# One block for the projection stage and the page steps, an earlier stick-breaking chain, and router weights turned by TensorE

## What is computed

```python
def stick_breaking(q, k, v, q_pos, k_pos):
    z = einsum('bqhd,bkhd->bhqk', q, k) * SCALE
    causal = k_pos[None, :] < q_pos[:, None]
    log_stay = where(causal, log_sigmoid(-z), 0.0)
    later = cumsum(log_stay, axis=3, reverse=True) - log_stay
    a = where(causal, exp(log_sigmoid(z) + later), 0.0)
    return einsum('bhqk,bkhd->bqhd', a, v)

def forgetting(q, k, v, cq, ck, q_pos, k_pos):
    z = einsum('bqhd,bkhd->bhqk', q, k) * SCALE + cq[..., :, None] - ck[..., None, :]
    p = softmax(where(causal, z, -inf), axis=-1)
    return einsum('bhqk,bkhd->bqhd', p, v)

def hier_moe(u, w_rg, b_rg, w_re, b_re, w_gate, w_up, w_down):
    lg = u @ w_rg + b_rg                      # 4 groups
    le = einsum('td,gde->tge', u, w_re) + b_re  # 4 x 8 experts
    ...
```

## Time and profile before

| | us |
|---|---|
| median of 3 runs | 1610.4 (1608.38 to 1613.99) |
| the profiled execution | 1617.14 |
| its span in the profile | 1615.2 |
| PE busy | 1275.5 (79%) |
| DVE busy | 668.7 (41%) |
| ACT busy | 230.6 (14%) |
| moved by DMA | 576.64 MB, 357 GB/s over the span |
| mean granted TensorE clock | 0.882 |

### The profile page before, as it was taken

How to read it: one execution, slowest core, us unless ns; L and a number is a source line. 1 busy time by engine, 2 the same in 40 slices (tenths; PEclk the granted TensorE clock), 3 DMA queues, 4 the chain that set the end, 5 groups by cost and what they waited for, 6 DMA issues and landing times. The chain is left out here.

```text
span 1615.2 us, 24640 instructions
## 1 busy us (share of the span) xinstructions
PE 1275.5 (79%) x7826; PEld 811.5 (50%) x7827; DVE 668.7 (41%) x4780; ACT 230.6 (14%) x454; POOL 62.4 (4%) x107
## 2 busy tenths in 40 slices
PE   5996679887969889847999776789867787767782
PEld 3775356655646656514777432355434444334451
DVE  3544655666557657659734654020100000000004
ACT  2100101212202213211010021010110001100011
POOL 1000000000000000001000000000010000000000
PEclk8998789899979989967999885799998889988997
DMA  9868599999989999999989899999999999999974
GB/s 329 235 221 325 176 397 394 397 396 394 357 334 379 395 366 395 389 388 371 360 335 361 316 364 353 411 377 411 422 399 381 381 388 388 372 375 382 369 332 167
DMA packets 188252, 576.64 MB, mean 357 GB/s; under 512 B 28697, under 2 KB 88906, under 8 KB 170218
## 3 DMA queue, kind: packets, MB, share of 16 engines
q1 hardware_dynamic: 116432, 507.82, 81.2%
q10 hardware_dynamic: 67282, 58.55, 11.0%
q0 software_dynamic: 4432, 9.05, 1.7%
HBM read 568.74 MB, written 17.77 MB: 363 GB/s over the span
## 5 line engine op out<-in xcount | busy, mean ns | idle before, releaser
L129 DVE CUSTOM_DVE_ANT_0 ws<-ws,xgT 128x128 f32<-128x128 f32 x1792 | 386.5, 281 | 90.2 <-issue 36.5
L1877 PE MATMUL bank<-ws,xgT 128*64 128x256 f32 x1024 | 260.4, 419 | 108.2 <-DMA ws<-in_w_expert_up 104.6
L932 PE MATMUL bank<-xn,ws 128*128 128x264 f32 x1152 | 297.0, 414 | 58.3 <-DMA ws<-in_w_in 58.3
L932 PEld LDWEIGHTS bank<-xn,ws 128*128 128x128 f32 x1152 | 228.0, 203 | 156.5 <-DMA ws<-in_w_in 66.9
L1879 PE MATMUL bank<-ws,xgT 128*64 128x256 f32 x1024 | 260.6, 419 | 0.0
L1877 PEld LDWEIGHTS bank<-ws,xgT 128*64 128x64 f32 x1024 | 152.9, 152 | 205.8 <-issue 120.5
L2076 DVE COPY gu<-bank 128x256 f32<-128x256 f32 x32 | 13.6, 424 | 391.0 <-PE bank L1879 391.0
L917 PE MATMUL bank<-ws,PR 128*32 128x512 f32 x1024 | 150.7, 668 | 21.2 <-DMA ws<-in_cache_fox_v 17.5
L1879 PEld LDWEIGHTS bank<-ws,xgT 128*64 128x64 f32 x1024 | 152.7, 152 | 0.0
L129 DVE DVE_READ_ACCUMULATOR2_ANT Z<- 128x1 f32 x1792 | 137.0, 76 | 0.0
L1898 PE MATMUL bank<-ws,hT 128*32 128x512 f32 x1024 | 115.7, 604 | 12.7 <-ACT xgT L1975 12.5
(11 more groups left out here) (409 smaller groups left out, 968.9 us busy)
## 6 DMA issues: line engine op xcount, KB each, us to landing
ws<-in_cache_sb_k SPq DMA_DIRECT2D x128, 512.0 KB, 8.1
ws<-in_cache_fox_k SPq DMA_DIRECT2D x128, 512.0 KB, 10.1
ws<-in_cache_sb_v SPq DMA_DIRECT2D x128, 512.0 KB, 7.6
ws<-in_cache_fox_v SPq DMA_DIRECT2D x128, 512.0 KB, 9.9
ws<-in_w_expert_gate SPq DMA_DIRECT2D x32, 2048.0 KB, 17.8
ws<-in_w_expert_up SPq DMA_DIRECT2D x32, 2048.0 KB, 24.9
ws<-in_w_expert_down SPq DMA_DIRECT2D x32, 2048.0 KB, 25.8
ws<-in_w_in ACTq DMA_DIRECT2D x16, 2048.0 KB, 30.2
```

Of the source, the lines that this page charges most:

```text
L129: ins = dve.tensor_tensor_reduce(k, k, qb[:, (g * H + h) * HD:(g * H + h + 1) * HD], 1.0, 0.0, ALU.mult, ALU.add, Z[:, n % 2, g, h, t:t + 1])
L932: mm = pe.matmul(out[:, 0:T], w[:, c, m * P:(m + 1) * P], xn[:, c, :], start=(c == 0), stop=(c == KC - 1))
L1877: pe.matmul(bank[2 * k][0:SLOTS, 0:256], lhs, ws[:, wg, c * 256:(c + 1) * 256], start=(c == 0), stop=(c == KC - 1))
```

## The change

1. The first block's streams become functions (`class start`) that each engine runs at the beginning of the second block. The meeting of the engines, the clearing of the first set of semaphores and the wait for the `lf` stores between the two go. The first set is cleared at the end of the merged block, so three sets are cleared there instead of two. The stores of `lf` move forward, behind query chunk 6, and are waited for in step 8.
2. The stick-breaking chain of sample 0 moves to the time when the fox half of its pages is being scored: the softplus on ACT stands behind `head(4)`, the sum and scan on DVE ahead of the fox half, the two sum matmuls on PE behind `head(6)`, `ts` behind the first fox half page, and its exponential on ACT behind the fox queries. The softmax part stays at the start of the steps. There PE first turns the maximum, then broadcasts sample 1's queries. POOL's clearing of `PR` runs once the gate logits are made.
3. The router weights are loaded by SP as rows (16 partitions with 4 KB each) ahead of the query chunks, and PE turns them with 36 small transposes; DVE copies them to `wr`. The gains also move to SP, ahead of the chunks; `wf`, `bf` and `br` are issued by ACT later.
4. Buffers of the first stage now lie inside those of the second (`blk`, `PR`, `osum`, `zs`, `zr`, `ts`, `zx`), and several semaphores are shared.

The diff, cut to the core:

```diff
@@ SP
                 for t in (2, 0, 1):
                     ...
                     sp.dma_start(xrow[0:n, t, :], src).then_inc(A[f"x{t}"], 16)
+                for i, (name, r0, r1) in enumerate((("norm_attn_g", 0, 16), ...)):
+                    sp.dma_start(grow[r0:r1, :], a[name][0].rearrange("(c p) -> c p", p=P)).then_inc(A["g_in"], 16)
+                for g in range(NG):
+                    sp.dma_start(wrow[g], a["w_router_expert"][0, g].rearrange("(c p) e -> c (p e)", p=P)).then_inc(A["wr_in"], 16)
+                sp.dma_start(wrow[4], a["w_router_group"][0].rearrange("(c p) g -> c (p g)", p=P)).then_inc(A["wr_in"], 16)
                 for n in range(4):
                     q_chunk(n)
...
                 q_chunk(6)
+                sp.wait_ge(A["fgc"], FG["lf"])
+                sp.dma_start(logf_p[0, 0]..., lf[:, 0:2, :]).then_inc(A["lst"], 16)
+                sp.dma_start(logf_s[0]..., lf[0:NB, 2, :]).then_inc(A["lst"], 16)
...
-                sp.wait_ge(A["lf"], 1)
-                sp.dma_start(logf_p[0, 0]..., lf[:, 0:2, :]).then_inc(A["lst"], 16)
-                sp.dma_start(logf_s[0]..., lf[0:NB, 2, :]).then_inc(A["lst"], 16)
-                sp.wait_ge(A["lst"], 32)
@@ ACT
                 head(4)
+                act.wait_ge(A["hused"], PAGES)
+                own.step(nc.scalar.activation(zs[:, :], Z[:, 0, 0, :, :]..., ACT.Abs, scale=SCALE))
+                own.step(nc.scalar.activation(zs[:, :], zs[:, :], ACT.Exp, scale=-1.0))
+                nc.scalar.activation(zs[:, :], zs[:, :], ACT.Ln, bias=1.0).then_inc(S["ssl"], 1)
                 head(5)
                 head(6)
                 partial(3)
                 act.wait_ge(S["bcast"], 1)
                 for i in range(2, 4):
                     nc.scalar.activation(qb[:, i * 512:(i + 1) * 512], bank[i][:, :], ACT.Copy).then_inc(S["qb"], 1)
+                act.wait_ge(S["pad"], 1)
+                act.wait_ge(S["ts"], 1)
+                nc.scalar.activation(PR[:, 0, :, 0:H]..., ts[:, :]..., ACT.Exp).then_inc(S["w"], 1)
@@ PE
+                pe.wait_ge(A["wr_in"], 16 * (NG + 1))
+                for e in range(NE):
+                    g, i = divmod(e, EPG)
+                    pe.transpose(bank[3][:, e * KC:(e + 1) * KC], wrow[g]...[:, i, :], ident[0:KC, 0:KC])
+                for g in range(NG):
+                    mm = pe.transpose(bank[2][:, g * KC:(g + 1) * KC], wrow[4]...[:, g, :], ident[0:KC, 0:KC])
                 pe.wait_ge(A["rc"], 1)
...
                 head(6)
+                pe.wait_ge(A["fgc"], FG["ctc"])
+                pe.wait_ge(S["ssp"], 1)
+                pe.matmul(bank[1][:, P:2 * P], tri_ge[:, :], sp_h[:, :, 1:PAGES + 1], start=True, stop=False)
+                pe.matmul(bank[1][:, P:2 * P], ones[:, :], run[:, :, 0:PAGES], start=False, stop=True).then_inc(A["fg"], 1)
                 partial(7)
...
-            pe.wait_ge(S["pad"], 1)
+            start.tensor(pe)
+            sample_max(0)
+            pe.wait_ge(A["q_evac"], 12)
             broadcast_queries(pe, S, bank[4:8], lastq, qpart, 1)
-            sample_max(0)
-            sample_sums(0)
+            pe.wait_ge(S["diag"], 1)
+            pe.matmul(bank[CH][:, 256:256 + H], ones[0:H, :], diag[:, :], start=True, stop=True).then_inc(S["C2"], 1)
@@ ACT, ahead of the steps
+            start.scalar(act)
+            act.wait_ge(S["zx"], 1)
+            nc.scalar.activation(PR[:, 1, :, 0:H]..., zx[:, :]..., ACT.Exp).then_inc(S["w"], 1)
             copy_queries(nc, act, S, bank[4:8], qb, 1)
-            sample_softplus(0)
-            act.wait_ge(S["pad"], 1)
-            sample_weights(0)
@@ DVE
+                own.step(dve.tensor_scalar(zr[:, :], z_sb, SCALE, 0.0, ALU.mult, ALU.max))
+                dve.wait_ge(S["ssl"], 1)
+                own.step(dve.tensor_tensor(sp_h[:, :, 1:PAGES + 1], zr..., zs..., ALU.add))
+                dve.tensor_tensor_scan(run..., seg..., sp_h..., 0.0, ALU.mult, ALU.add).then_inc(S["ssp"], 1)
                 for i in range(PAGES, 2 * PAGES):
                     score_half(i)
+                    if i == PAGES:
+                        dve.wait_ge(A["fg"], FG["c2s"])
+                        dve.scalar_tensor_tensor(out=ts[:, :], in0=z_sb, scalar=SCALE, in1=bank[1][:, P:2 * P], ...).then_inc(S["ts"], 1)
-        done_with(nc, A)
...
         attention_and_route(...)
+        done_with(nc, A)
         done_with(nc, S)
         done_with(nc, C)
@@ DVE, ahead of the steps
+            start.vector(dve)
+            dve.wait_ge(S["kused"], PAGES)
+            own.step(dve.scalar_tensor_tensor(out=zx[:, :], in0=flat(Z[:, 0, 1, :, :]), scalar=SCALE, in1=FB[:, 0, :], ...))
+            dve.tensor_reduce(mxp[:, :], by_head(zx[:, :]), AX, ALU.max).then_inc(S["mx"], 1)
+            dve.wait_ge(S["mxT"], 1)
+            own.step(dve.tensor_reduce(m8[:, :], bank[CH][0:H, 0:P], AX, ALU.max))
+            dve.tensor_scalar(diag[:, :], ident[0:H, 0:H], m8[:, 0:1], None, ALU.mult).then_inc(S["diag"], 1)
+            dve.wait_ge(S["C2"], 1)
+            own.step(dve.tensor_copy(MX[:, 0, :], bank[CH][:, 256:256 + H]))
+            dve.tensor_tensor(by_head(zx[:, :]), by_head(zx[:, :]), over(MX[:, 0, :], PAGES), ALU.subtract).then_inc(S["zx"], 1)
+            for p in range(PAGES, LEAD):
+                score_page(dve, S, kring, qb, Z, p)
```

More of the change, by code:

```diff
@@ new lines, in hybrid_step @@
+        sp_h = sb("sp_h", [P, H, PAGES + 1], where=bctx)
+        run = sb("run", [P, H, PAGES + 1], where=bctx)
+        ts = sb("ts", [P, H * PAGES], where=bctx)
+        zx = sb("zx", [P, H * PAGES], where=bctx)
+        tri_gt, tri_le, later, grow = ts, zr, zx, zs[0:48, :]
+        lfr, LFT, totb = (blk[:, i * 1024:(i + 1) * 1024] for i in range(3))
+        totb = totb.rearrange("p (h n) -> p h n", h=H)
+        rstd = osum[:, 0:T]
+        prf = PR[:, :, :, :].rearrange("p g t r -> p (g t r)")
@@ L282, in chunk, with sync @@
             return ws[:, Q_SLOT[n], :].rearrange("p (c n) -> p c n", n=256)
[L284 to L286 removed]
+        class start:
+            def sync(sp):
                 def q_chunk(n):
                     c0 = (n // 4) * 3 * H * HD + (n % 4) * 256
[L289 removed]
+                    sp.dma_start(chunk(n), w_in[:, :, c0:c0 + 256]).then_inc(W[Q_SLOT[n]], 16)
                 def key_half(i):
```

216 lines of the change are left out of this document (109 added, 107 removed).

## The result

The changed kernel takes **1603.3 us** (median of 9 runs, 1595.0 to 1608.4); the kernel before took 1614.1 beside it (9 runs, 1608.4 to 1621.6). The ratio is 0.993 with a 95% interval of 0.9902 to 0.9958. The direction was right; the size was not: 1592.4 was forecast, outside the range that ended at 1599.5. Of the 10.9 us between forecast and measurement, 3.7 are the base: the three runs from which I started (1610.4) lay under the 1614.1 of the nine. The other 7.2 are gain that did not come: 10.8 us instead of 18.0.

A forecast was written before the change was run, and what follows sets the result against it. Transfers were taken to set the pace, with a hole in them at the block boundary. 20.1 - 0.5 - 0.9 - 0.7 = 18.0 us, and 1610.4 - 18.0 = 1592.4 us, range 1586 to 1599.5.

The forecast's parts named there:

- The boundary: Between the first block's last product and the steps: without the wait, key page 23 is issued 20.1 us earlier.
- The chain: Stick-breaking chain moved under the fox half: hidden there, but two sum matmuls on PE cost 0.5 us, bounds 0 and 1.
- The front: Loads ahead of the query chunks: their bytes cost 0.9 us, bounds 0 and 3.2; the transposes net 0.
- The end: End of the merged block: clearing a third semaphore set costs 0.7 us, bounds 0 and 1.5.
- The base: Starting time of the kernel before, from which the gain was subtracted: a median of 1610.4 us.
- The whole gain at the end: From the boundary to the kernel's end: the early gain less three costs, 18.0 us, arrives whole; chance 0.80.
- part of the gain is given back: Rival: a later stage returns part of the gain, leaving 8 to 12 us, 1598 to 1602; chance 0.08.

The follow-up runs named there:

- Experiment 4: Changed kernel with the `lf` stores back behind value page 3 and SP, PE and DVE waiting for them: 1619.19 us, 1.0014 of the kernel before.
- experiment 6: Changed kernel with the stick-breaking chain of sample 0 back at the start of the steps, between and behind pages 16 and 17: 1604.99 us, 0.993 of the kernel before.
- Experiment 3: Changed kernel with the gains and router row loads issued by ACT instead of SP, transposes kept: 1599.23 us, 0.9901 of the kernel before.
- experiment 2: Changed kernel with the old front: gains and small-piece router loads on ACT, no transposes: 1599.75 us, 0.9908 of the kernel before.
- turned_in_wait: Changed kernel with sample 0's weight sum early, row loads behind key half 3, transposes behind the first sample's maxima; page 23 issued at 171.27 us.
- experiment 7: Changed kernel with gains on ACT, row loads behind key half 3 and transposes between `head(2)` and `head(3)`: 1605.85 us, 0.9932 of the kernel before.
- den_and_clear: Changed kernel with sample 0's weight sum early and the first block's semaphores not cleared at the end; PE's idle stretch there is 3.60 us.
- turned_and_clear: turned_in_wait with the first block's semaphores not cleared at the end of the steps; no measured time stated.
- same_again: The changed kernel run again unaltered, for a second profile: 1599.27 us, 0.9915 of the kernel before.
- experiment 5: Changed kernel with sample 0's softmax denominator summed on DVE ahead of key pages 16 to 19: 1598.1 us, 0.9898 of the kernel before.
- experiment 9: Last value-projection weight load issued by SP behind value page 68, not by ACT: changed kernel 1596.11 us, kernel before with the same edit 1614.16 us.
- all_in_order: Changed kernel with all 16 projection weight loads of the steps issued by SP behind value pages: 1593.98 us, 0.987 of the kernel before.

## Why the prediction was right in kind and wrong in size

- **The boundary (20.1 us)**: right, and slightly better. From DVE's last product to page 16 the changed kernel takes 7.7 us (8.7 forecast), and from page 16 to the issue of page 23 14.4 (14.4 forecast). Experiment 4 shows that the store wait held this time: put back, it delays page 23 by 17.4 us and the end by 17.7.
- **The chain (0.5)**: right. PE's four instructions take 0.64 us, and no wait was added. The 1.9 us for DVE's operations between pages 16 and 19 was also right (experiment 6), but not by the sum given: eight of 0.29 and a scan of 0.44 make 2.8. The timeline has six small ones and the scan there, 1.9 together.
- **The front (0.9, bounds 0 and 3.2)**: a mis-sized term. Chunk 3 came 3.1 us later, and by the use of chunk 4 PE was 4.1 behind (67.00 against 62.94). I had priced the row loads by their bytes at 329 GB/s and weighed their issue time as the other bound. Experiment 3 shows the issue time to be worth nothing. What was missing is that while the row loads run the DMA engines are fully busy at half the rate: 2.1 us. Of the 4.1 us, 2.9 are left at DVE's last product (150.55 against 147.63). With the front as it was (experiment 2) page 23 comes no earlier, because DVE and the clock of the broadcast take the time back; with rows and transposes late (`turned_in_wait`) it comes 1.4 us earlier. So the front explains little of the missing 7.2 us. The Trainium skill, page "SBUF — State Buffer", section "Door 1: The DMA port swizzle", says that the rate of a load depends on how many of the 16 SBUF ports its partitions reach, and by its table partitions 0 to 15 reach four. The 164 GB/s go with that, but no run here changed the number of partitions, so the reason for the low rate is not shown. I had weighed only the rule about the issuing engine, and experiment 3 agrees with that one.
- **The end (0.7)**: right, 0.73.
- **The base**: my sum gave a gain, and I set it against the median of three runs. All 93 runs of the kernel before have the median 1615.1, so three runs were 4.7 us low. The scatter of one kernel's executions (here 1608 to 1629) belonged in the range as an error of the base, and I had counted 3 us for it in all.
- **The whole gain at the end (18.0)**: the step that failed. The sum let the 20.1 us, less three small costs, arrive at the end undiminished ("a time gained here should reach the end whole"), and gave the rival *part of the gain is given back* 0.08. The first nine runs show 10.8 us, inside that rival's 8 to 12. The early lead is not what was wrong (18.2 us at page 23, 18.7 forecast); the loss lies between there and the end. Over both batches, the changed kernel's 15 runs against the 26 of the kernel before beside them, the mean gain is 12.8 us (95% by resampling the runs: 10.1 to 15.6). So about 5 us of the 18 are missing even when the error of the base is taken out.

I had argued against the rival that "every load there waits for a page used, and those uses all shift". That is true of the pages. It is not true of the sixteen projection weight loads on ACT's queue, which share the DMA engines with the pages, stand in no order with them, and land some 31 us after their issue (median). Where the last one lands late, PE waits 7 to 9 us, no page comes free, and the queues can run dry. The wait is there in the first profile, in those of experiments 2, 4, 6 and 7, of `den_and_clear`, `turned_in_wait` and `turned_and_clear`, and in both of the kernel before. It is not in `same_again`. Since both kernels have this stall, it explains how two executions of one kernel come to differ by 4 to 6 us, and not yet why the changed kernel gains less than forecast.

Are these loads the place of the missing 5 us? For the three pairs in which they are halved or in order, taken together, the mean gain is 16.6 us (14.2 to 18.9), 3.8 more than the 12.8 (0.2 to 7.4 by resampling). In the last of these pairs a lead of 17.5 to 21 us over the twin is there from page 6 to the fourth gate load. That speaks for them. Against them: three kernels of one batch that leave the loads as they were (`same_again` and experiments 2 and 3) have a mean gain of 15.2 us (12.9 to 17.9), which is not set apart from 16.6; experiment 5 has 17.1. Much of the difference is thus the low gain of the first nine runs, which no second batch repeated. A second rival is that the merged block loses something late whatever its lead: experiment 4, set against the other merged kernel, loses nothing of its 17.4 us, and set against the kernel before it is some 3 us behind. The hand-over to the experts is where this would be looked for: 0.3 to 6.4 us of lead go there between the first and the fourth gate load in the profiles of the merged kernels, and at most 2.4 in those of the kernels of the old form. No run was made for it. So the mechanism at the boundary was right, and that its gain comes to the end diminished is measured; which of these takes the rest stays open.

## What to carry to other kernels

A wait that holds a chain of loads is worth what its stretch of the DMA line shows, and here the shift of the first loads behind it was forecast to half a microsecond. Whether it reaches the end is another question: list the queues that are not chained to the one that was moved and what waits for each of their loads, and take a second profile of both kernels before a difference between two profiles is called a loss. Here a stall that seemed to belong to the changed kernel was in the second profile of the kernel before as well. Price a load by the rate at which loads of its shape run, not by its bytes alone. And give the base its own error: three runs of a kernel whose executions scatter by 10 us do not fix its median to better than a few.

## What the runs showed of the hardware that was not expected

- **A load lands sooner after its issue on the queue of the loads that it competes with.** The last 2 MB of weights, in pieces of 1 KB, landed after 34.0 us on ACT's queue beside pages in pieces of 4 KB on SP's (27.4 us in `same_again`), and after 10.9 us on SP's queue behind a page (experiment 9). Over all such loads the median falls from 31.4 to 21.3 us. The lists of DMA issues from 190 to 700 us of the changed kernel, and over 200 to 700 us of `all_in_order` (KB each, median us to landing):

```profile
ws<-in_cache_sb_v SPq DMA_DIRECT2D x72, 512.0 KB, 9.4
ws<-in_w_in ACTq DMA_DIRECT2D x15, 2048.0 KB, 31.4
```

```profile
ws<-in_cache_sb_v SPq DMA_DIRECT2D x73, 512.0 KB, 8.4
ws<-in_w_in SPq DMA_DIRECT2D x15, 2048.0 KB, 21.3
```

  The Trainium skill, page "DMA: Bandwidth & Descriptors", section "Queues, rings and completion order", says that a DMA engine takes turns between the queues that have work, a packet at a time. If the packets of one queue are small and those of the other large, the queue with the small ones would get the smaller share. The landing times here agree with that, but no run changed the size of the pieces, so that the size is the reason is not shown.
- **Small transposes let the clock fall.** After 36 transposes of 16x16 without a gap, the granted clock was 0.60 in the window behind them (experiment 7), so PE ran mostly at its level of 1.2 GHz there, and the next two heads took 1.4 us more. PE was busy in every window of that stretch, so being busy did not keep the clock here.
